# Half-row norms, an earlier turn of mixer parts, and a reordered projection in the second block of a two-block fp32 transformer kernel

## The reference

```python
hc = modulate(rms_norm_2(x_ctx, norm1_g[l]), cmod[0], cmod[1])
if last:  # layer 1: the context gives keys and values only
    pkv = hc @ w_in[l][:, COL_K:COL_C]
else:     # layer 0: the context goes through the whole layer
    pa_c, q_c, k_c, v_c, pc_c = project(hc, P, None)
    ...
hl = modulate(rms_norm_2(x_lat, norm1_g[l]), sh1, sc1)
pa, q, k, v, pc = project(hl, P, rope)      # one product with w_in, 5 groups of 512 columns
k_all = jnp.concatenate([k, k_c], axis=1)
v_all = jnp.concatenate([v, v_c], axis=1)
o = blocked_diff_attn(q, k_all, v_all, lam)                   # two softmaxes, their difference
x_lat = x_lat + g1 * mixer_merge(pa, o, pc, P, lam_init)      # pa: gated part, pc: 31-tap filter
h2 = modulate(rms_norm_2(x_lat, norm2_g[l]), sh2, sc2)
x_lat = x_lat + g2 * conv_ffn(h2, P)
```

## Time and profile before

| | before |
|---|---|
| median of 3 runs | 2391.27 us (2388.01 to 2393.47) |
| profiled execution | 2390.97 us |
| its span in the profile | 2389.3 us |
| around the span | 1.7 us |
| PE, DVE, ACT, POOL busy | 94%, 59%, 44%, 13% |
| granted PE clock, mean | 0.967 |

### The profile page before, as it was taken

How to read it: one execution, slowest core, us unless ns; L and a number is a source line. 1 busy time by engine, 2 the same in 40 slices (tenths; PEclk the granted TensorE clock), 3 DMA queues, 4 the chain that set the end, 5 groups by cost and what they waited for, 6 DMA issues and landing times. The chain is left out here.

```text
span 2389.3 us, 32051 instructions
## 1 busy us (share of the span) xinstructions
PE 2238.6 (94%) x12368; PEld 1826.2 (76%) x12368; DVE 1409.1 (59%) x2231; ACT 1045.2 (44%) x1743; POOL 306.1 (13%) x313
## 2 busy tenths in 40 slices
PE   8999899999999999898999978699999999779988
PEld 6777677778777777676888866588888887659987
DVE  4655485544456554854555698655555237776764
ACT  4445444444445455454444445433232224554442
POOL 0005421000000054220000162000000001500000
PEclk9999999999999999999999989799999999889999
DMA  7645333465656453344655421223333335134554
GB/s 237 199 162 175 119 124 128 163 216 199 231 197 198 164 174 125 124 146 172 219 180 178 132 71 53 63 71 114 106 106 104 110 95 159 59 115 154 178 184 141
DMA packets 171846, 349.33 MB, mean 146 GB/s; under 512 B 11825, under 2 KB 23217, under 8 KB 171697
## 3 DMA queue, kind: packets, MB, share of 16 engines
q1 hardware_dynamic: 171696, 347.29, 44.5%
HBM read 346.19 MB, written 1.05 MB: 145 GB/s over the span
## 5 line engine op out<-in xcount | busy, mean ns | idle before, releaser
L843 DVE TENSOR_TENSOR wlo<-wraw,whi 128x1024 fp32r<-128x1024 f32 (+1 forms) x535 | 647.9, 1224 | 665.7 <-ACT whi L1040 663.3
L1040 ACT ACTIVATE whi<-wraw 128x1024 fp32r<-128x1024 f32 (+1 forms) x552 | 558.7, 1027 | 570.0 <-PE psum L1797 267.5
L1797 PE MATMUL psum<-whi,act_h 128*128 128x512 f32 (+2 forms) x1424 | 575.5, 404 | 16.0 <-DVE modT L1389 6.5
L1797 PE MATMUL psum<-wlo,act_h 128*128 128x512 f32 (+2 forms) x1424 | 555.3, 390 | 0.0
L1797 PE MATMUL psum<-whi,act_l 128*128 128x512 f32 (+2 forms) x1424 | 554.5, 389 | 0.0
L1797 PEld LDWEIGHTS psum<-whi,act_h 128*128 128x128 f32 x1424 | 273.4, 192 | 83.0 <-issue 20.8
L1797 PEld LDWEIGHTS psum<-whi,act_l 128*128 128x128 f32 x1424 | 272.7, 192 | 57.3
L1797 PEld LDWEIGHTS psum<-wlo,act_h 128*128 128x128 f32 x1424 | 273.8, 192 | 48.6
L1797 PE MATMUL psum<-act_h,whi 128*128 128x512 f32 (+1 forms) x704 | 242.8, 345 | 10.7 <-DVE wlo L843 3.8
L1797 PE MATMUL psum<-act_l,whi 128*128 128x512 f32 (+1 forms) x704 | 238.3, 339 | 0.0
L1797 PE MATMUL psum<-act_h,wlo 128*128 128x512 f32 (+1 forms) x704 | 238.1, 338 | 0.0
(11 more groups left out here) (272 smaller groups left out, 2736.0 us busy)
## 6 DMA issues: line engine op xcount, KB each, us to landing
wraw<-in_w_in SPq DMA_DIRECT2D x136, 512.0 KB, 4.1
wraw<-in_w_gate SPq DMA_DIRECT2D x104, 512.0 KB, 4.1
wraw<-in_w_mod_pieces SPq DMA_DIRECT2D x96, 512.0 KB, 4.8
wraw<-in_w_ffn_in SPq DMA_DIRECT2D x80, 512.0 KB, 4.4
wraw<-in_w_ffn_out SPq DMA_DIRECT2D x44, 512.0 KB, 4.3
wraw<-in_w_down SPq DMA_DIRECT2D x44, 512.0 KB, 3.9
wraw<-in_w_val SPq DMA_DIRECT2D x40, 512.0 KB, 4.1
wraw<-in_w_branch SPq DMA_DIRECT2D x32, 512.0 KB, 4.8
```

The costliest lines, as they stand in the source:

```text
L843: eng.tensor_tensor(wlo[:, i, 0:st.n, 0:st.w], wraw[:, st.s % RING_W, 0:st.n, 0:st.w], whi[:, i, 0:st.n, 0:st.w].bitcast(F32), ALU.subtrac ...
L1040: nc.scalar.activation(whi[:, d % RING_S, 0:st.n, 0:st.w], wraw[:, s % RING_W, 0:st.n, 0:st.w], ACT.Copy).then_inc(sem("slab_rounded"), 1)
L1797: return nc.tensor.matmul(out, lhsT, rhs, start=start, stop=stop)
```

## The change

It works on the second block, in four parts.

1. **Half norms.** Each norm of layer 0 and the first of layer 1 are done for lat and ctx apart. The last three slabs of the product ahead of a norm are multiplied for lat first (`parts`, `late=3`), then for ctx (`slab_rest`), and the lat half of the norm is put among the ctx matmuls (`ending`). The first four slabs behind the norm are multiplied for one half first (`early=4`) and for the other behind it, so the other half of the norm is put among them. At the entry of the block the ctx half, which depends on inputs alone, is done among the last slabs of the first block. `warm` stays only at layer 1's second norm.
2. **modsplit** takes two channel pieces of one half at a time: DVE scales one, ACT the other, ACT rounds both, and DVE's subtraction of the last step comes behind the scaling of the next (`held_rows`).
3. **Order** of the projection: keys, queries, filter input, gate input, values. The filter's taps start behind `qkT2`, and in layer 0 the last 10 taps of ACT and POOL go into the attention (`late`).
4. **ysplit** of the gated part (k = 0, 1) and the filtered part (k = 6, 7) stand in the attention's last steps; the other four behind slab 0 and 1 of w_out.

The loads of the gate rows (`load_gates`) move behind the first projections, with a semaphore of their own. Rounding is tied to when a ring slot is free (`rounds`).

```diff
@@ gemm
+            if c == 0 and at < early or a + w == width and at >= len(order) - late:
+                st.parts = parts
+                held.append(Step(kind="slab_rest", rest=st, banks=banks))
...
+            if held and (last or c == 0 and at == early - 1):
+                steps += held
+                held = []
@@ plan_second
+    def ending(root, splits):
+        two = pl.steps[-2:]
+        del pl.steps[-2:]
+        pl.steps += [root] + two[:1] + splits[:2] + two[1:]
+        return Step(kind="res_rest", rest=two[1].rest)
...
-            pl.steps.append(warm(pl, 40 if l == i == 0 else 24))
...
-        ready, ss = norm(0, 4, l > 0)
+        if l == 0:
+            root, c, of_ctx = norm(0, ctx, pl.tick("norm2_sums", 4))
+            for at, st in zip((9, 12, 13, 14, 15, 16), [Step(kind="ctx_sums", n=now), root] + c):
+                at = pl.steps.index(pl.last_out[at])
+                pl.steps[at:at] = [st]
+            root, a, of_lat = norm(0, lat, pl.tick("norm2_sums", 4), first=True)
+            ss = [(0, root), (3, a[0]), (3, a[1]), (4, a[2]), (4, a[3])]
+            ready = [of_ctx, of_lat]
+        else:
+            root, a, ready = norm(0, lat, now - 2)
+            rest = ending(root, a)
+            root, b, of_ctx = norm(0, ctx, now)
+            ss = [(0, rest), (1, a[2]), (1, a[3]), (2, root), (3, b[0]), (3, b[1]), (4, b[2]), (4, b[3])]
...
-        gq = project(C_Q, T, ready)
-        gc = project(C_C, T)
-        gk = project(C_K, 4)
+        gk = project(C_K, 4, ready, parts=[lat, ctx] if l else [ctx, lat], early=4)
+        gq = project(C_Q, T)
+        gc = project(C_C, T)
+        moved = len(gk) - KD // SLAB_K
...
-        for i, (g, tiles, at) in enumerate(((gq, T, 4), (gk, 4, 12))):
+        for i, g, tiles, at in ((1, gk, 4, 4), (0, gq, T, 8)):
...
-        others = ss + [(8, cglu), (9, ct)] + list(zip((9, 10, 11, 12, 16, 17, 18, 19), wide))
-        others += [(10 + n, st) for n, st in enumerate(slow)]
-        others += qk + [(16, qkt), (16, gelu), (18, aln[0]), (19, aln[1])]
+        others = qk + [(12, qkt), (12, cglu), (13, ct)] + list(zip((13, 14, 15, 16, 17, 18, 19, 19), wide))
+        late = slow[7:] if l == 0 else []
+        others += [(14 + (n if l == 0 else n // 2), st) for n, st in enumerate(slow) if st not in late]
+        others += [(16, gelu), (18, aln[0]), (19, aln[1])]
+        others = ss + [(at + moved, st) for at, st in others]
...
+            stream += late[:2]
+            del late[:2]
...
+        att[next_ys:next_ys] = ss[2:4]
+        att[first_ys:first_ys] = ss[:2]
+        pl.steps += interleave(stream, att)
@@ vector
+            def lower_rows(st):
+                m, h = turned_rows(st)
+                need(dve, drained(st.bank))
+                dve.tensor_tensor(h(act2_l), m, h(act2_h).bitcast(F32), ALU.subtract).then_inc(sem("mod_lo"), 1)
```

More of the change, by code:

```diff
@@ L175, in riding, with gemm @@
             + slabs[-2:-1] + splits + slabs[-1:])
-def gemm(pl, weight, layer, act, tiles, nk, col0, width, evac, row0=0, kt0=0, ready=(), turned=False, order=None, **more):
+def gemm(pl, weight, layer, act, tiles, nk, col0, width, evac, row0=0, kt0=0, ready=(), turned=False, order=None, parts=None, early=0, late=0,
+         **more):
     steps = []
@@ L441, in plan_second @@
         pl.x_start[l] = pl.now("x_new")
-        def norm(i, tiles, summed):
-            n = pl.tick("norms2")
-            if not summed:
-                pl.tick("norm2_sums", 2 * tiles)
-            pl.add("norm2", n=n, tiles=tiles, x=pl.now("x_new"), sums=pl.now("norm2_sums"), first=not summed)
-            out = pl.tick("xn_out", tiles)
-            pl.steps.append(warm(pl, 40 if l == i == 0 else 24))
-            ss = [Step(kind="modsplit", l=l, i=i, k=k, tiles=tiles, bank=pl.misc(), waits=[("xn_out", out)],
-                       hi=pl.tick("split2_hi"), lo=pl.tick("mod_lo"),
-                       halves=[("mod_half", pl.tick("mod_half"))] if tiles == 4 else []) for k in range(KD)]
-            return {st.k: [("mod_lo", st.lo)] for st in ss}, between(ss)
@@ L476, in plan_second @@
         cglu = Step(kind="cglu", l=l, tiles=T, waits=landed(gc))
+        qkt = Step(kind="qkT2", l=l, tiles=T, sq0=pl.now("qk_sq") + T + 4, banks=[pl.misc() for _ in range(8)])
         ct = Step(kind="cT", l=l, tiles=T, banks=[pl.misc(), pl.misc()])
@@ L488, in plan_second @@
             qk += [(at + 1 + min(t, 2), Step(kind="qk_scale", t=t, **more)) for t in range(tiles)]
-        qkt = Step(kind="qkT2", l=l, tiles=T, sq0=pl.now("qk_sq"), banks=[pl.misc() for _ in range(8)])
         gelu = Step(kind="gelu", l=l, tiles=T, waits=landed(ga))
@@ L613, in build @@
         st.split = (name, pl.tick(name))
+    used, waiting = -1, []
+    for st in pl.steps:
+        if st.kind == "slab":
+            waiting.append(st.s + AHEAD)
+        if st.kind in ("slab", "slab_rest"):
+            while waiting and (waiting[0] >= len(slabs) or slabs[waiting[0]].evac == "mod" or slabs[waiting[0]].d - RING_S <= used):
+                st.rounds.append(waiting.pop(0))
+            of = st.rest or st
+            if of.evac != "mod" and (st.rest or not st.parts):
+                used = of.d
     with ExitStack() as ctx:
@@ L955, in _ @@
             for st in pl.steps:
[L956 to L957 removed]
+                for s in st.rounds:
+                    if s < len(slabs) and slabs[s].pool:
+                        lower_halves(pool, slabs[s])
                 if st.kind == "slab" and st.evac == "proj" and st.last and st.br:
@@ L1051, in _ @@
                     act.wait_ge(sem("params_landed"), 16 * PARAMS)
+                for s in st.rounds:
+                    round_slab(s)
+                if st.kind == "slab" and st.parts and st.evac != "res":
+                    continue
+                if st.kind == "slab_rest" and st.rest.evac != "res":
+                    st = st.rest
                 if st.kind == "slab":
-                    round_slab(st.s + AHEAD)
                     if not st.last:
@@ L1307, in _ @@
                     dve.wait_ge(sem("params_landed"), 16 * PARAMS)
+                for s in st.rounds:
+                    split_slab(s)
+                if st.kind == "slab" and st.parts and st.evac != "res":
+                    continue
+                if st.kind == "slab_rest" and st.rest.evac != "res":
+                    st = st.rest
                 if st.kind == "slab":
-                    split_slab(st.s + AHEAD)
                     if not st.last:
```

281 lines of the change are left out of this document (174 added, 107 removed).

## The result

| | before | changed |
|---|---|---|
| median of 4 runs each | 2392.37 us (2388.01 to 2395.22) | 2364.30 us (2358.92 to 2369.54) |
| ratio, 95% interval | | 0.9888 (0.9869 to 0.9907) |
| a second comparison | 2394.04 us (13 runs) | 2360.55 us (4 runs), ratio 0.9854 (0.9832 to 0.9876) |
| span of the profiled execution | 2389.3 us | 2364.0 us |

The change makes the kernel 28 us faster in the first comparison and 33 in the second. The forecast was 2346, in a range of 2326 to 2370: inside the range, but some 15 to 18 us too fast.

What follows compares the result with a forecast made beforehand. PE's weight stream was taken as the floor, with the vector engine close to a bound. The terms 22 - 5 + 6 + 5 + 12 + 4 + 0.5 = 44.5 us came off 2391, giving 2346, range 2326 to 2370.

Steps and rivals of the forecast that it cites:

- Layer 0's entry and projection: Second block, from block 1's last product to layer 0's first scores: 155.6 us becomes 130, DVE's bound; 22 us won after ctx turns.
- The late taps: Attention of layer 0: ten POOL taps, 14.5 us, now run in it and cost DVE 5 us.
- 6 won: End of layer 0's attention: slab 0 of w_out covers PE's 4.3 us wait, and 16 turns, 1.9 us, fill waits inside.
- the norm's 5: Norm behind layer 0's mixer: 14.5 us before, 9.3 after with half norms, so 5 us won.
- The term of 12: Layer 1's entry and projection: 117.0 us becomes 105, so 12 us won, between 5 and 27.
- The 4 us for denser taps: Layer 1's projection: POOL's taps, shut into fewer slabs, keep DVE company more densely and cost 4 us.
- The attention of layer 1 and the norm behind it: Layer 1: 4 us won at the attention's end, under slab 0 and by 8 turns leaving; 0.5 at the norm.
- Only the norms win: Rival, 16%: DVE needs as long after the keys as before; only norms and attention ends win, 24 us, giving 2367.
- 6 at layer 0's entry: Term of the norms rival: 6 us won by the norm at layer 0's entry if DVE wins nothing else there.
- 8 at layer 1's: Term of the norms rival: 8 us won by the norm at layer 1's entry.
- Slower by POOL: Rival, 5%: POOL's taps stop DVE for their whole time, not a third; 28 us slower, 2419.
- The signs that were named: Second block, if right: no `ident` matmuls before keys; `qkT2` waits under 3 and around 12 us; stretches near 130 and 105.

## Why the prediction was right and wrong

**Layer 0's entry and projection, 22 forecast, 20.9 measured.** The stretch took 131.2 us where 130 was forecast, the norm's 15 us went, no wait stands at `qkT2`, and the first scores' wait lies where it was forecast (7.44 us and one of 3.7 ahead of it, for some 10). That DVE sets this time, and PE's own bound is 119 to 120, was shown too: with POOL's additions cut short the stretch is 120.6, and PE is busy 120.1 of it. But the 130 was partly luck. It was 107.7 us of DVE's work and 22.5 of its idle time; measured are 103.4 and 27.6, so two misses of 4 to 5 us cancel. The sum of the work hid two more misses: the prediction took 5 off the taps for the ten of POOL's that leave, and nothing off the rest. The taps stayed at 34.5 (34.2 before), since those that are left are packed, and some 10 us came from the scalings, rotations and weight subtractions that POOL no longer slows, although already showed such a scaling at 1.75 for 0.69.

**The late taps, forecast as 5 us back in the attention.** Measured are 2.9 there and 3.7 behind it, 6.6 in all. The size was near, the place half wrong: the prediction counted only what POOL costs DVE, not that the filtered part's norm is pushed onto the last units of the attention. So of "6 won" at its end, 7.2 were won by the turns and 3.7 lost to the taps, and of the norm's 5 about 2.7 came.

**Layer 1, the step that failed.** The term of 12 measured 8.2, less 1.8 for the lat turns that now lie in w_down: 6.4. The prediction counted those turns, 3.8 us at the block's entry, only in layer 0; in layer 1 it put all 64 behind w_down. Of the 5.6 us that this lacks to 12, 3.4 are the residual of ctx rows ahead of the lat scaling, which it named nowhere; moving it won them, and what is left stays open. The keys' phase took 31.7 us, with DVE busy in 16.8, where 29.4 with 19 of work was counted: the time was there, the order was wrong. Over the whole stretch DVE's work came out at 82.7 and not 86.7, and its idle time at 26.1 and not 17.9. `qkT2` waits 5.9 and not 12, but what it gave up stands in waits on `wlo` during the queries (1.3, 2.0, 0.8). The 4 us for denser taps were right, 30 taps took 18.5 us before and 22.4 in the change, but the scalings and rotations of queries and keys took some 3 less, and a part of the norm's work lies in w_down.

**The attention of layer 1 and the norm behind it, 4.5 forecast, 2.1 measured.** The 4.9 us of wait did not lie under slab 0 alone; 2.6 remain, because the output's own scaling is late.

**The last product lost 2.1 us** in the two traces of the change (68.8 and 67.7). In ten of the fourteen traces of this study it took 66.1 to 66.2, and in the other two 67.5 and 67.8, the latter with the order alone on the kernel before. These four have 0.95 or 0.96 of the clock there and the ten others 0.98; in the change's trace much of the half clock lies at the head, 0.64 over the first 8 us. So the loss goes with the clock and not with the product's own work; why the clock was low in both traces of the change is not shown.

**Rivals.** "Only the norms win" gave 2367, nearer to the measured 2364.30 and 2360.55 than the forecast of 2346 was. The range holds the result because it was widened for this rival; the forecast's own terms at their bounds, 2331 to 2360, do not. The kernel with the halves but the old order took 2366.74. Both agreements are luck in part. The order does shorten both stretches, by 10.8 and 3.3 us on top of the halves; the change comes near the rival because the order loses 6.4 again behind the first one. And of the rival's terms, 6 at layer 0's entry measured 10.1 with the halves alone (13.8 less the 3.7 of ctx turns), and 8 at layer 1's measured 3.1 (4.9 less 1.8). "Slower by POOL" had the threshold at three quarters of POOL's time; measured on DVE's taps is 29% in the change (12.2 of 41.6 us) and 45% when packed (21.3 of 47.4).

The sum of 44.5 is 13 too high: 5.6 in layer 1's entry, 2.4 behind it, 1.8 net at the end of layer 0's attention and its norm, 1.1 at the first term, 2.1 of clock at the end.

**The signs that were named.** Layer 0's came: no `ident` matmuls ahead of the keys, under 3 us at `qkT2`, some 10 at the first scores, and a stretch near 130. Layer 1's did not: `qkT2` waits 5.9 and not 12, and the stretch is 108.9 and not 105. Of the signs of being wrong, the slow taps (1.15 us in the mean, under 1.3) and waits on `wlo` in the keys' phase did not come; those on `wlo` stand behind it.

## What to carry to other kernels

Cut the time into stretches by instructions that both kernels have, and compare these over two traces: here the stretches repeated to 0.2 us while the whole varied by several. Then read the granted clock of each stretch before giving a difference of one or two us to the edit. When a norm or a product is cut in halves, look on the vector engine at what the second half puts ahead of the first half's next step; the same edit won 3.4 us at one norm and lost 1.7 at another. Work moved out of a crowded stretch is not saved until one has seen what stands behind it in the list, here a norm that came 5.4 us later against the scores and cost 3.7. And where two engines slow each other, moved work relieves its old neighbours and loads its new ones: here the scalings of queries and keys got shorter and the taps did not.

## What the runs showed of the hardware

- A DVE tap with inputs in SBUF beside a POOL addition took up to 1.756 us, where alone it took 0.721 and the shortest of POOL's 1.043, and where both had taps to do each came out at one every 1.6 us: they take turns. On the whole 30 taps took 22.3, 34.5 or 43.6 us, by how many of POOL's lay beside them.
- The same first block ended up to 9.3 us apart in eleven traces (1311.9 to 1321.2), while stretches of the second block that were unchanged agreed to 0.2 us (131.1 to 131.2 us from the end of block 1 to the first reduction, in eight traces of seven kernels). In the two traces of the change the drift stood in different places.
- The granted clock of the first stretch was 1.00 with POOL's additions cut, 0.98 in the change, 0.95 without late taps, 0.93 with the halves alone and 0.96 before, where warm matmuls fill the norm. PE was idle for 0.4, 9, 16, 16 and 19 us of it.
- The attention of layer 1 took 23.5 to 23.8 us at a granted clock of 1.00, 25.0 to 25.3 at 0.93 and 26.3 to 26.4 at 0.87, over fourteen traces of twelve kernels with DVE's work the same to 2.4 us.
